# Differential heads: one fp32 product with the values in place of three on split operands

## The chip, the cores and the metric

The kernel runs on one core of a Trainium2 chip. The metric is the device time of one execution in microseconds. The core has a matrix engine (TensorE, PE in the profile; its weight loads have a row of their own, PEld), a vector engine (VectorE, DVE), a scalar engine (ScalarE, ACT), GpSimd (POOL) and a queue engine (SyncE, SP). Each works off its own list of instructions in order, and they wait for one another on semaphores.

## What is computed

A decoder block on x of 2048 x 1024 in fp32: RMSNorm, one input projection, two kinds of causal attention side by side, an output projection, and an MLP. There are 8 forgetting heads ("fox" below) of width 64 and 4 differential heads ("diff" below) with two score matrices each and values of width 128. The part that the change touches, from the reference:

```python
s = jnp.einsum('bqhnd,bkhnd->bhnqk', q_i, k).astype(jnp.float32) * scale
s = s + bias[None, :, None]
s = jnp.where(mask, s, -jnp.inf)
p = jax.nn.softmax(s, axis=-1)
a = p[:, :, 0] - lam * p[:, :, 1]
o = jnp.einsum('bhqk,bkhd->bqhd', a.astype(v.dtype), v)
o = rmsnorm(o, g_sub) * (1.0 - lam_init)
```

## The kernel before

There are four stages: the projection (to about 575 us of the profiled execution), the attention (to about 1376 us), the output projection and the MLP. fp32 products are made on TensorE from operands in the type fp32r: a number is split into a high part `hi`, which is the number copied into an fp32r tile, and a low part `lo`, the difference; the product is hi by hi, hi by lo and lo by hi, and each of the three is one matmul instruction.

The projection (`project`) makes a job for every 128 x 512 piece of its output. ScalarE copies the piece out of PSUM as `hi` (L534), VectorE subtracts to get `lo` (L598), and ScalarE's queue stores both. For the values there are 16 jobs of fox heads and 16 of diff heads; `vals` holds 256 columns for each row of a head, hi in the first 128 and lo in the other 128 for a diff head.

The attention (`attend`) goes through 8 units, fox and diff in turn: one unit is two fox heads or one diff head. A unit is cut into blocks of 512 queries (J = 0 to 3; a diff unit takes them in the order 1, 3, 2, 0), and a block needs keys up to its own end. For each block and each 128 queries the steps are

- score: TensorE, queries by keys into one of two PSUM buffers `at_ps_s` (L1462, the mask L1465, L1468);
- max: VectorE, the negated row maximum (L1361), and where a row has over 1024 keys the smaller of two (L1365) and on ScalarE a correction (L1293);
- exp: ScalarE, into `at_probs` (L1313); the score buffer is free after that;
- in diff blocks chain and mix: VectorE works out the factor of the second softmax (L1382 to L1390), and the second matrix is scaled and added to the first on VectorE (L1399, L1404), or on GpSimd (L1235 to L1251), or by ScalarE and GpSimd (L1320, L1322, L1222, L1226);
- turn: TensorE transposes 128 keys of up to 512 queries into one of the three PSUM buffers of the ring `at_ps_t`, in up to four matmuls of 128 columns (L1486);
- hi: ScalarE copies the turned tile into one of the four tiles `at_p_hi` (L1331);
- lo: VectorE subtracts, into `at_p_lo` (L1370); this also gives the ring's buffer back (semaphore `x_free`);
- pv: TensorE multiplies with the values into `at_ps_o`: two matmuls in a fox block (L1501, L1502), three in a diff block (L1504, L1505, L1506), all of up to 512 columns.

At the end of a diff block ScalarE squares the output (L1346), TensorE takes the mean with four matmuls of one column in fp32 (var, L1513), which take a place of the same ring, and VectorE (L1434, o_var) gives that place back. There are 480 turned tiles, 320 of fox blocks and 160 of diff blocks; the 160 are 112 of 512 queries and 16 each of 384, 256 and 128.

The order of all this is not written by hand. `attention_steps` hands each step to `Walk` with an engine, a holding time, a time to its result, an urgency and what it waits for; `Walk.order` lists them as the engines would come to them. A step's holding time is a number of us per column: 0.0009 for the pv of a fox block, 0.00135 for that of a diff block. The list is made once, when the program is built; on the chip each engine follows it in order.

## Time and profile before

| | |
|---|---|
| median of 3 runs | 2805.71 us (2801.96 to 2806.47) |
| the profiled execution | 2801.12 us |
| its span | 2799.4 us |
| granted TensorE clock, mean | 0.998 |
| TensorE busy over the span | 97% |
| VectorE busy over the span | 63% |
| ScalarE busy over the span | 48% |

The profile gives, for one execution, the busy time of each engine in each stretch, groups of equal instructions with their mean duration and the idle time before them with what ended it, and lists of waits. The duration of a matmul in it runs from its start to the arrival of its last result, so matmuls overlap in the records: what one costs the engine is the distance from its start to the start of the next.

### The profile page before, as it was taken

Reading aid. Unit: us, or ns where it says so; the run is one execution under the profiler, and the core shown is the slowest. Engines: PE = TensorE matmul, PEld = TensorE weight load, DVE = VectorE, ACT = ScalarE, POOL = GpSimd, SP = SyncE. Lnnn points to the kernel's source line nnn. Section 1 sums busy time; section 2 is a strip of 40 time slices with the busy share of each in tenths; the row PEclk is TensorE's granted clock in tenths of the full one; section 3 lists DMA queues with packets and bytes.
Section 4 is the critical chain, followed back from the end, with each engine's and each line's share of the span. In section 5 each row is a group of like instructions: output and inputs, shape, how many; then the busy total and the mean of one; then the engine's idle time right before and its main releaser. Section 6 shows DMA issues by size and latency. Waiting matters only on the chain.

```text
span 2799.4 us, 36795 instructions
## 1 busy us (share of the span) xinstructions
PE 2725.3 (97%) x13362; PEld 2253.3 (80%) x13362; DVE 1756.6 (63%) x2495; ACT 1344.5 (48%) x2413; POOL 629.6 (22%) x558
## 2 busy tenths in 40 slices
PE   8999999989999999999999999999999999999998
PEld 6888888878787787877788788888888888888887
DVE  6211111169889889899846778887777544435567
ACT  5121111168788788788523545464444433322233
POOL 5220021026746646556411100000000000000012
PEclk9999999999999999999999999999999999999999
DMA  5443343464434514414346755565345555546566
GB/s 190 131 153 101 104 136 113 144 148 98 105 83 97 128 52 118 123 41 120 106 128 217 260 204 199 186 237 201 134 149 196 180 186 209 185 159 224 203 219 240
DMA packets 287660, 434.49 MB, mean 155 GB/s; under 512 B 19648, under 2 KB 134592, under 8 KB 287488
## 3 DMA queue, kind: packets, MB, share of 16 engines
q1 hardware_dynamic: 241664, 368.41, 42.4%
q10 hardware_dynamic: 45056, 63.05, 6.2%
q8 instruction: 101, 1.65, 0.2%
q0 software_dynamic: 768, 0.79, 0.1%
q14 instruction: 71, 0.58, 0.1%
HBM read 280.27 MB, written 151.91 MB: 154 GB/s over the span
## 4 chain that ended last, share of the span: by engine, by line
PE 68%; DVE 5%; ACT 4%; issue 3%; POOL 0%; ACTq 0%; POOLq 0%; DVEq 0%
PE ml_ps L2845 7%; PE ml_ps L2843 7%; PE ml_ps L2844 7%; PE ml_ps L2813 7%; PE ml_ps L2815 7%; PE ml_ps L2816 7%; PE at_ps_t L1486 5%; PE at_ps_s L1462 4%; PE at_ps_s L1468 3%; PE mo_acc L1801 2%; PE mo_acc L1803 2%; PE mo_acc L1802 2%; PE at_ps_o L1501 2%; PE at_ps_o L1502 2%; ACT at_probs L1313 2%
## 5 line engine op out<-in xcount | busy, mean ns | idle before, releaser
L1361 DVE TENSOR_REDUCE at_nmax<-at_ps_s 128x1 f32<-128x1024 f32 (+7 forms) x384 | 346.6, 906 | 37.0 <-PE at_ps_s L1468 34.8
L2813 PE MATMUL ml_ps<-ml_h_hiM,ml_w_hi 128*128 128x512 f32 x896 | 349.1, 390 | 1.0 <-DVE ml_t L2635 0.9
L2816 PE MATMUL ml_ps<-ml_h_hiM,ml_w_lo 128*128 128x512 f32 x896 | 348.7, 389 | 0.0
L2815 PE MATMUL ml_ps<-ml_h_loM,ml_w_hi 128*128 128x512 f32 x896 | 348.7, 389 | 0.0
L2845 PE MATMUL ml_ps<-ml_b_hi,ml_a_lo 128*128 128x512 f32 x896 | 348.6, 389 | 0.0
L2844 PE MATMUL ml_ps<-ml_b_lo,ml_a_hi 128*128 128x512 f32 x896 | 348.6, 389 | 0.0
L2843 PE MATMUL ml_ps<-ml_b_hi,ml_a_hi 128*128 128x512 f32 x896 | 348.6, 389 | 0.0
L598 DVE SCALAR_TENSOR_TENSOR pj_out_sb<-pj_acc,pj_out_sb 128x512 fp32r<-128x512 f32 x96 | 66.4, 691 | 424.1 <-ACT pj_out_sb L534 424.1
L1370 DVE TENSOR_TENSOR at_p_lo<-at_ps_t,at_p_hi 128x512 fp32r<-128x512 f32 x480 | 280.0, 604 | 35.8 <-ACT at_p_hi L1331 32.7
L1331 ACT ACTIVATE at_p_hi<-at_ps_t 128x512 fp32r<-128x512 f32 x480 | 248.5, 533 | 87.6 <-PE at_ps_t L1486 48.0
L2490 POOL TENSOR_SCALAR ml_ss<-ml_ss 128x1 f32<-128x1 f32 x16 | 17.6, 1099 | 1183.7 <-ACT ml_junk L2583 1183.4
L1486 PE MATMUL at_ps_t<-at_ident_r,at_probs 128*128 128x128 f32 x1632 | 249.7, 275 | 14.9 <-DVE at_p_lo L1370 8.1
L534 ACT ACTIVATE pj_out_sb<-pj_acc 128x512 fp32r<-128x512 f32 x96 | 57.4, 598 | 422.8 <-PE pj_acc L705 268.8
L1313 ACT ACTIVATE at_probs<-at_ps_s,at_nmax 128x1024 f32<-128x1024 f32 (+7 forms) x256 | 237.4, 927 | 42.3 <-DVE at_nmax L1361 37.5
L1486 PEld LDWEIGHTS at_ps_t<-at_ident_r,at_probs 128*128 128x128 f32 x1632 | 193.8, 141 | 57.9 <-DVE at_p_lo L1370 16.0
L1462 PE MATMUL at_ps_s<-at_k,at_q 128*128 128x512 f32 (+3 forms) x640 | 211.5, 395 | 18.2 <-ACT at_probs L1313 14.4
L1215 POOL TENSOR_TENSOR at_probs<-at_probs,at_corr 128x1024 f32<-128x1024 f32 x96 | 181.9, 1894 | 152.8 <-ACT at_corr L1293 152.8
L2270 ACT ACTIVATE ml_b_hi<-ml_b_raw 128x1024 fp32r<-128x1024 f32 x56 | 59.4, 1061 | 307.2 <-issue 164.9
L1468 PE MATMUL at_ps_s<-at_k,at_q 128*128 128x512 f32 (+3 forms) x640 | 203.6, 383 | 0.0
L2813 PEld LDWEIGHTS ml_ps<-ml_h_hiM,ml_w_hi 128*128 128x128 f32 x896 | 168.2, 188 | 37.2 <-issue 1.7
L2125 ACT ACTIVATE ml_w_hi<-ml_w_sum 128x1024 fp32r<-128x1024 f32 x80 | 84.8, 1061 | 234.0 <-DVE ml_w_sum L2107 233.0
L2816 PEld LDWEIGHTS ml_ps<-ml_h_hiM,ml_w_lo 128*128 128x128 f32 x896 | 168.2, 188 | 35.0
(264 smaller groups left out, 5981.3 us busy)
## 6 DMA issues: line engine op xcount, KB each, us to landing
ml_a_raw<-ua SPq DMA_DIRECT2D x112, 512.0 KB, 3.9
qk<-pj_out_sb ACTq DMA_DIRECT2D x64, 512.0 KB, 2.8
ml_w_raw<-in_w_up_dram SPq DMA_DIRECT2D x64, 512.0 KB, 5.1
ua<-ml_t SPq DMA_DIRECT2D x128, 256.0 KB, 2.6
ml_b_raw<-in_w_down_dram SPq DMA_DIRECT2D x56, 512.0 KB, 4.9
at_q<-qk SPq DMA_DIRECT2D x96, 256.0 KB
at_k<-qk SPq DMA_DIRECT2D x96, 256.0 KB
ua<-ml_x SPq DMA_DIRECT2D x96, 256.0 KB, 2.6
```

The source lines that it names most:

```text
L1313: act.activation(out, ps_s[:, sc.g % 2, 0:sc.width], ACT.Exp, bias=bias, accum_out=rsum[:, par, sc.a, s, sc.part:sc.part + 1]).then_inc(ex ...
L1361: dve.tensor_reduce(nmax[:, par, sc.a, s, sc.part:sc.part + 1], ps_s[:, sc.g % 2, 0:sc.width], AX.X, ALU.max, negate=True).then_inc(maxed, 1)
L1370: dve.tensor_tensor(p_lo[:, t.n % PRING, t.off:512], ps_t[:, at % TRING, t.off:512], f32(p_hi[:, t.n % PRING, t.off:512]), ALU.subtract).t ...
L1462: pe.matmul(ps_s[:, sc.g % 2, at:at + width], q2[:, n, sc.s, q], k2[:, slot, sc.s, 0:width], start=True, stop=False)
L1468: last = pe.matmul(ps_s[:, sc.g % 2, at:at + width], q1[:, n, sc.s, q], k1[:, slot, sc.s, 0:width], start=False, stop=True)
L1486: last = pe.transpose(ps_t[:, at % TRING, a * P:(a + 1) * P], probs[:, key:key + P], ident)
L2813: pe.matmul(to, hi, h_hi[m][:, k, :], start=begins and k == 0, stop=False, skip_group_check=not begins)
L2815: pe.matmul(to, hi, h_lo[m][:, k, :], start=False, stop=False, skip_group_check=not begins)
L2816: last = pe.matmul(to, lo, h_hi[m][:, k, :], start=False, stop=k == 3, skip_group_check=not begins)
L2843: pe.matmul(to, hi, b_hi[b % 4][:, k, :], start=begin, stop=False)
L2844: pe.matmul(to, hi, b_lo[b % 4][:, k, :], start=False, stop=False)
L2845: last = pe.matmul(to, lo, b_hi[b % 4][:, k, :], start=False, stop=end)
```

## The change

In the diff blocks the turned probabilities are copied once, by ScalarE, in plain fp32 into a tile `p_whole`, which lies where `p_lo` lies. The step lo is left out there, so the ring's buffer is given back by ScalarE's copy (`hi_ready`). The product with the values is one matmul instruction in fp32 on the fp32 values instead of three in fp32r. The values of the diff heads are no longer split in the projection: VectorE copies a piece out of PSUM whole, ScalarE does nothing for it, and half as many bytes are stored and loaded. Fox blocks keep both parts. Two semaphores now tell of a free ring buffer, and the waits are counted apart (`hi_at`, `x_no`). In the planner the diff step lo is gone, and the holding time of the diff pv is 0.0018 us a column instead of 0.00135.

```diff
+def split(job):
+
+    return job.what == "qk" or (job.what == "val" and job.n == FOX)
...
+        with ExitStack() as shared:
+            r = Room(nc, shared, "atw")
+            r.sb("p_hi_place", [P, 4, 512])
+            self.p_whole = r.sb("p_whole", [P, 4, 512])
...
+                    used = 256 if job.n == FOX else P
+                    act.dma_start(vals[job.n, :, job.rb * P:(job.rb + 1) * P, 0:used].rearrange("i p c -> p i c"),
+                                  src.rearrange("p (i c) -> p i c", c=256)[:, :, 0:used]).then_inc(stored[job.out % OR], 16)
...
+                elif not split(job):
+                    dve.wait_ge(multiplied, m + 1)
+                    dve.wait_ge(stored[job.out % OR], 16 * (job.out // OR))
+                    dve.tensor_copy(f32(out_view(job, 0)), acc_view(job)).then_inc(evacuated, 1)
...
-            ring.append(("lo", t))
+            ready = ("lo", t) if fox else ("hi", t)
+            ring.append(ready)
...
-            walk.step("lo", t, "DVE", 0.07 + 0.00104 * width, at + RUSH["lo"], [("hi", t)], 0.15 + 0.00104 * width, line="ring")
-            cost = (0.0009 if fox else 0.00135) * width
+            if fox:
+                walk.step("lo", t, "DVE", 0.07 + 0.00104 * width, at + RUSH["lo"], [("hi", t)], 0.15 + 0.00104 * width,
+                          line="ring")
+            cost = (0.0009 if fox else 0.0018) * width
...
-                    act.activation(p_hi[:, t.n % PRING, t.off:512], ps_t[:, at % TRING, t.off:512], ACT.Copy)\
-                       .then_inc(hi_ready, 1)
...
+                    to = (p_whole if blocks[t.b].kind == DIFF else p_hi)[:, t.n % PRING, t.off:512]
+                    act.activation(to, ps_t[:, at % TRING, t.off:512], ACT.Copy).then_inc(hi_ready, 1)
...
+            def wait_free(at):
+                if at in hi_at:
+                    pe.wait_ge(hi_ready, hi_at[at])
+                else:
+                    pe.wait_ge(x_free, x_no[at])
...
-                        pe.matmul(out, v[:, 0:P], p_hi[:, ring, t.off:512], start=start, stop=False)
-                        pe.matmul(out, v[:, P:2 * P], p_hi[:, ring, t.off:512], start=False, stop=False)
-                        last = pe.matmul(out, v[:, 0:P], p_lo[:, ring, t.off:512], start=False, stop=t.end)
+                        last = pe.matmul(out, f32(v[:, 0:P]), p_whole[:, ring, t.off:512], start=start, stop=t.end)
```

The planner lists the steps of a diff unit in another order with this. On TensorE, in the second diff unit, from the mean of the first finished block (`at_mean`) on, before the change; `at_ps_s` are scores, `at_ps_t` turned tiles, `at_ps_o` the product with the values:

```order
L1486 MATMUL at_ps_t<-at_ident_r,at_probs 128x128 x12
L1513 MATMUL at_ps_t<-at_mean,at_o_sq 128x1 x4
L1462 MATMUL at_ps_s<-at_k,at_q 128x512 x2
L1468 MATMUL at_ps_s<-at_k,at_q 128x512 x2
L1486 MATMUL at_ps_t<-at_ident_r,at_probs 128x128 x4
L1462 MATMUL at_ps_s<-at_k,at_q 128x384
L1465 MATMUL at_ps_s<-at_mask_q,at_ident_r 128x128
L1468 MATMUL at_ps_s<-at_k,at_q 128x384
L1486 MATMUL at_ps_t<-at_ident_r,at_probs 128x128 x4
L1504 MATMUL at_ps_o<-at_p_hi,at_v_sb 128x512
L1505 MATMUL at_ps_o<-at_p_hi,at_v_sb 128x512
L1506 MATMUL at_ps_o<-at_p_lo,at_v_sb 128x512
```

The same place in the changed kernel:

```order
L1522 MATMUL at_ps_t<-at_ident_r,at_probs 128x128 x12
L1547 MATMUL at_ps_t<-at_mean,at_o_sq 128x1 x4
L1540 MATMUL at_ps_o<-atw_p_whole,at_v_sb 128x512
L1522 MATMUL at_ps_t<-at_ident_r,at_probs 128x128 x11
L1540 MATMUL at_ps_o<-atw_p_whole,at_v_sb 128x512
L1498 MATMUL at_ps_s<-at_k,at_q 128x512 x2
L1504 MATMUL at_ps_s<-at_k,at_q 128x512 x2
L1498 MATMUL at_ps_s<-at_k,at_q 128x384
L1501 MATMUL at_ps_s<-at_mask_q,at_ident_r 128x128
L1504 MATMUL at_ps_s<-at_k,at_q 128x384
```

One product and three more turned tiles now stand ahead of the two scores. On VectorE, at the same block's `at_var`, before and after the change:

```order
L1370 TENSOR_TENSOR at_p_lo<-at_ps_t,at_p_hi 128x512
L1361 TENSOR_REDUCE at_nmax<-at_ps_s 128x1
L1365 TENSOR_REDUCE at_top<-at_nmax 128x1
L1370 TENSOR_TENSOR at_p_lo<-at_ps_t,at_p_hi 128x512 x2
L1361 TENSOR_REDUCE at_nmax<-at_ps_s 128x1 x2
L1365 TENSOR_REDUCE at_top<-at_nmax 128x1
L1434 SCALAR_TENSOR_TENSOR at_var<-at_squares,at_ps_t 128x4
```

With the change, at that place:

```order
L1420 TENSOR_SCALAR at_factor<-at_factor,at_corr 128x1
L1393 TENSOR_REDUCE at_nmax<-at_ps_s 128x1 x2
L1397 TENSOR_REDUCE at_top<-at_nmax 128x1
L1464 SCALAR_TENSOR_TENSOR at_var<-at_squares,at_ps_t 128x4
```

The three subtractions are gone, and the maxima stand one behind the other.

## Rows read from the trace of the kernel before

**Rows 1.** Busy us by stretch; columns: stretch, its length, PE, PEld, DVE, ACT, POOL, PEclk, DMA

```profile
450.00:560.00 110.00, 110.00 (x487) 91.10 (x486) 13.83 (x20) 11.96 (x20) 8.37 (x3) 1.00 0.40 125
800.00:900.00 100.00, 96.29 (x573) 79.42 (x572) 92.98 (x156) 86.81 (x185) 57.50 (x43) 1.00 0.32 76
900.00:1000.00 100.00, 93.04 (x568) 77.58 (x568) 86.83 (x180) 77.21 (x181) 58.49 (x46) 1.00 0.47 118
```

**Rows 2.** The same view, short stretches of one diff unit's products with the values

```profile
904.00:912.00 8.00, 6.62 (x38) 5.29 (x38) 6.99 (x15) 7.70 (x16) 5.53 (x4) 1.00 0.22 66
912.00:920.00 8.00, 7.36 (x39) 5.70 (x38) 7.72 (x16) 7.01 (x16) 5.32 (x5) 1.00 0.54 143
926.00:932.00 6.00, 4.91 (x34) 4.29 (x33) 5.41 (x15) 4.71 (x10) 4.83 (x4) 1.00 0.00 0
...
944.00:950.00 6.00, 5.96 (x35) 4.82 (x34) 5.68 (x14) 4.99 (x14) 5.68 (x4) 1.00 0.34 85
950.00:956.00 6.00, 4.86 (x27) 3.74 (x26) 5.56 (x14) 2.58 (x8) 3.50 (x5) 1.00 1.04 230
...
968.00:974.00 6.00, 6.00 (x36) 5.01 (x35) 4.40 (x8) 4.32 (x14) 0.00 (x0) 1.00 1.02 244
```

**Rows 3.** Waits in 904:986; engine, line waited for: us in total, times, longest us

```profile
PE at_ps_s L1462 <- ACT at_probs L1313: 2.5, 5, 1.2
...
PE at_ps_t L1513 <- DVE at_p_lo L1370: 1.6, 2, 1.1
...
PE at_ps_t L1486 <- DVE at_probs L1404: 1.1, 1, 1.1
```

**Rows 4.** PE in order of time, four pieces; columns: start us, us, engine, line, operation

```profile
922.19 0.22 PE L1465 MATMUL at_ps_s<-at_mask_q,at_ident_r 128*128 128x128 f32 x1
922.25 0.45 PE L1468 MATMUL at_ps_s<-at_k,at_q 128*128 128x512 f32 x1
...
925.27 1.47 PE L1486 MATMUL at_ps_t<-at_ident_r,at_probs 128*128 128x128 f32 x12
...
935.80 0.40 PE L1504 MATMUL at_ps_o<-at_p_hi,at_v_sb 128*128 128x512 f32 x1
936.03 0.39 PE L1505 MATMUL at_ps_o<-at_p_hi,at_v_sb 128*128 128x512 f32 x1
936.26 0.40 PE L1506 MATMUL at_ps_o<-at_p_lo,at_v_sb 128*128 128x512 f32 x1
```

**Rows 5.** PE in order of time: one diff block's narrow products, and a mean

```profile
1372.96 0.34 PE L1504 MATMUL at_ps_o<-at_p_hi,at_v_sb 128*128 128x384 f32 x1
...
1373.50 0.28 PE L1504 MATMUL at_ps_o<-at_p_hi,at_v_sb 128*128 128x256 f32 x1
...
1373.86 0.22 PE L1504 MATMUL at_ps_o<-at_p_hi,at_v_sb 128*128 128x128 f32 x1
...
1374.14 0.62 PE L1530 MATMUL at_ps_t<-at_ident_r,at_row 128*128 128x128 f32 x4
1374.99 1.05 PE L1513 MATMUL at_ps_t<-at_mean,at_o_sq 128*128 128x1 f32 x8 [0.23 <-ACT at_o_sq L1346]
```

**Rows 6.** Groups of instructions in 560:1400; count, then busy us, mean ns, idle before

```profile
L1504 PE MATMUL at_ps_o<-at_p_hi,at_v_sb 128*128 128x512 f32 x112 | 49.5, 442 | 0.1
L1513 PE MATMUL at_ps_t<-at_mean,at_o_sq 128*128 128x1 f32 x128 | 16.0, 246 | 7.0 <-DVE at_p_lo L1370 6.3 <-ACT at_o_sq L1346 0.7
```

**Rows 7.** The page's costliest groups: the copies, the subtractions, the projection's evacuation

```profile
L598 DVE SCALAR_TENSOR_TENSOR pj_out_sb<-pj_acc,pj_out_sb 128x512 fp32r<-128x512 f32 x96 | 66.4, 691 | 424.1 <-ACT pj_out_sb L534 424.1
L1370 DVE TENSOR_TENSOR at_p_lo<-at_ps_t,at_p_hi 128x512 fp32r<-128x512 f32 x480 | 280.0, 604 | 35.8 <-ACT at_p_hi L1331 32.7
L1331 ACT ACTIVATE at_p_hi<-at_ps_t 128x512 fp32r<-128x512 f32 x480 | 248.5, 533 | 87.6 <-PE at_ps_t L1486 48.0
```

**Rows 8.** DMA issues: count, KB each, median us to landing

```profile
vals<-pj_out_sb ACTq DMA_DIRECT2D x32, 512.0 KB, 2.9
at_v_sb<-vals SPq DMA_DIRECT2D x32, 512.0 KB, 3.9
```

More of the change, by code:

```diff
@@ L221, in project @@
         splits_after[m].append(z)
-    hi_no = {m: sum(1 for job in jobs[:m + 1] if job.what in ("qk", "val")) for m in range(len(jobs))}
+    hi_no = {m: sum(1 for job in jobs[:m + 1] if split(job)) for m in range(len(jobs))}
     carry_job = next(m for m, job in enumerate(jobs) if job.what == "carry")
@@ L529, in _ @@
                 if job.out is not None:
-                    if job.what != "logit":
+                    if split(job):
                         act.wait_ge(multiplied, m + 1)
@@ L1048, in attend @@
             ring += 1
+    hi_no, hi_at, x_no, his, frees = {}, {}, {}, 0, 0
+    for (what, arg), at in ring_at.items():
+        if what == "turn":
+            his += 1
+            hi_no[arg.n] = his
+        if what == "turn" and blocks[arg.b].kind == DIFF:
+            hi_at[at] = his
+        else:
+            frees += 1
+            x_no[at] = frees
     last_turn = {t.b: t for t in turns}
@@ L1082, in attend @@
         k1, k2, q1, q2, p_hi, p_lo = keep.k1, keep.k2, keep.q1, keep.q2, keep.p_hi, keep.p_lo
+        p_whole = keep.p_whole
         k_loaded, q_loaded = keep.k_loaded, keep.q_loaded
@@ L1130, in attend @@
         last_turned = max(turns, key=lambda t: ring_at["turn", t])
+        last_copy = max(n for n, (what, arg) in enumerate(steps) if what in ("hi", "lo") and arg is last_turned)
         last_spread = max(pairs, key=lambda pair: ring_at["spread", pair[0].qb])[0].qb
@@ L1176, in sync @@
                         sp.wait_ge(p_used, max(t.n for t in turns if blocks[t.b].u == held and t.j // 4 == p) + 1)
[L1177 to L1178 removed]
+                    used = 256 if u % 2 == FOX else P
+                    sp.dma_start(f32(v_sb[:, k_slot(u, p), :, 0:used]),
+                                 vals[u % 2, u // 2, 512 * p:512 * p + 512, 0:used].rearrange("(t k) c -> k t c", k=P))\
                       .then_inc(v_loaded[k_slot(u, p)], 16)
@@ L1288, in scalar @@
             first_hi = next(arg for what, arg in steps if what == "hi")
-            for what, arg in steps:
+            for n, (what, arg) in enumerate(steps):
+                if n == last_copy + 1:
+                    then()
                 if what == "corr":
@@ L1330, in scalar @@
                         act.wait_ge(p_used, t.n - PRING + 1)
-                    act.activation(p_hi[:, t.n % PRING, t.off:512], ps_t[:, at % TRING, t.off:512], ACT.Copy)\
-                       .then_inc(hi_ready, 1)
-                    if t is last_turned:
-                        then()
+                    to = (p_whole if blocks[t.b].kind == DIFF else p_hi)[:, t.n % PRING, t.off:512]
+                    act.activation(to, ps_t[:, at % TRING, t.off:512], ACT.Copy).then_inc(hi_ready, 1)
                 elif what == "o_half":
@@ L1355, in link @@
                     dve.wait_ge(chained, links[0])
-            for what, arg in steps:
+            for n, (what, arg) in enumerate(steps):
+                if n == last_copy + 1:
+                    then()
                 if what == "max":
@@ L1368, in vector @@
                     t, at = arg, ring_at["turn", arg]
-                    dve.wait_ge(hi_ready, t.n + 1)
+                    dve.wait_ge(hi_ready, hi_no[t.n])
                     dve.tensor_tensor(p_lo[:, t.n % PRING, t.off:512], ps_t[:, at % TRING, t.off:512],
                                       f32(p_hi[:, t.n % PRING, t.off:512]), ALU.subtract).then_inc(x_free, 1)
-                    if t is last_turned:
-                        then()
                 elif what == "chain":
@@ L1531, in tensor @@
                     last.then_inc(x_ready, 1)
-        return Attention(sync, gpsimd, scalar, vector, tensor, len(scores), ring_at["turn", last_turned] + 1, ring, scored,
+        return Attention(sync, gpsimd, scalar, vector, tensor, len(scores), ring_at["turn", last_turned] + 1, frees, scored,
                          exped, x_ready, x_free, p_used, o_free)
```

21 lines of the change are left out of this document (9 added, 12 removed).

## The prediction

> **What bounds the kernel now.** I read the busy time by stretch first, since the change touches two places only: the evacuation of the diff values in the projection, and the diff units of the attention. In the projection the matrix engine is busy for all 110 us of a stretch in which VectorE is busy for 13.83 and ScalarE for 11.96 [rows 1]: there only TensorE's work counts, and the change leaves it as it is. The attention repeats every 200 us, one fox and one diff unit. Its fox half (800 to 900 us) has PE 96.29, DVE 92.98, ACT 86.81; its diff half (900 to 1000 us) 93.04, 86.83, 77.21 [rows 1]. So no engine has much room, and TensorE has least.
>
> Inside the diff half the reader is to see three kinds of stretches [rows 2]. From 904 to 920 us TensorE is idle by 2.0 of 16 us while ScalarE (7.70 of 8) and then VectorE (7.72 of 8) are full: the loop of score, max and exp sets the pace. From 926 to 932 and from 950 to 956 TensorE loses 1.1 us each. From 944 to 950 and from 968 to 974, and in all from 938 to 986 but for some 1.6 us, TensorE is full: there its own work is the time. The list of waits names what it waited for over 904 to 986 us: 2.5 us for ScalarE's exp, 1.6 us where a mean waits for the subtraction `p_lo`, 1.1 us for VectorE's mix, 5.2 us in all [rows 3]. That is a small store of idle time, and it is what the change can win on TensorE's side.
>
> **The price of the product before.** Three fp32r matmuls of 512 columns start at 935.80, 936.03 and 936.26 [rows 4]: 0.231 us apart, 0.693 us for the three. The narrow ones start 0.54 us apart for the three of 384 columns, 0.36 for 256 (1373.50 to 1373.86) and 0.28 for 128 (1373.86 to 1374.14) [rows 5]. A diff unit has 28 full turned tiles (a quarter of the 112 in [rows 6]) and 4 of each narrow width: 28 x 0.693 + 4 x (0.54 + 0.36 + 0.28) = 19.4 + 4.7 = 24.1 us.
>
> **The price of the product after.** No row has an fp32 matmul of this width, so it is bounded. First, how many pieces: the mean is the one fp32 product in the attention that is no transposition. The code issues 16 x 4 = 64 of them, and the trace has 128 [rows 6], eight for each group of four [rows 5]. So one fp32 matmul is two pairs of a weight load and a matmul, and three fp32r matmuls become two pieces. The question is what a piece of 512 columns takes.
>
> - The low end: a piece goes as fast as an fp32r matmul, 0.231 us. Two are 0.46 us and a unit is 16 us, 8 us less than now, 32 us over the four units.
> - The nearest row for an fp32 operand that moves: 128 columns of it in a transposition. Twelve of these take 1.47 us, of which the last record is 0.27: 1.20 / 11 = 0.109 us each [rows 4]. An fp32r matmul of 128 columns has its follower 0.06 us behind it (922.19 to 922.25) [rows 4]. At 0.109 us per 128 columns a piece of 512 is 0.436 and two are 0.872 us. Then a unit is 28 x 0.872 + 4 x (0.654 + 0.436 + 0.218) = 24.4 + 5.2 = 29.6 us: 5.5 us more than now, 22 us over four units.
> - The high end: each piece also waits for its own load, another 0.11 us, which is what a piece of one column takes in the mean ((1.05 - 0.25) / 7 = 0.114 [rows 5]). That is 1.09 us for a full tile, some 38.5 us a unit, 14.4 us more than now and 57 us over four.
>
> The transposition's 0.109 could be its weight load alone, since the one-column piece takes as long; that keeps the low end alive. I take 0.872: it is the row with the same type and the same kind of operand, and halving the pace on full fp32 fits a split in two pieces better than two full-precision operands at the price of two fp32r passes would. So TensorE gets **22 us** more work.
>
> The Trainium skill, in "FP8 and Floating Point Precision", section TensorE Precision Notes, says that true fp32 takes four passes through the array. At the spacing of the fp32r rows, four would be 0.924 us for a full tile, and my estimate by that page is 7.5 us a unit, 30 us over four; no run here shows it yet.
>
> **What of it lies on the path.** From 938 us on, where most of a unit's products with the values stand, TensorE is full, so a longer product moves all behind it. Ahead of that TensorE waits at times, but for other engines that are waited for after the product as well; the product is not what fills those waits. I count the 22 us whole and look for relief apart.
>
> **What goes.** VectorE loses 160 subtractions. The group of 480 is busy for 280.0 us [rows 7]; a third is 93 us, 23 us of the 87 that VectorE is busy in a diff half. By itself this is off TensorE's path; it counts through the waits. The mean's wait of 1.6 us a unit ends with `p_lo`, since the ring's place comes back with ScalarE's copy: I take all of it. The waits for the mix and for exp, 1.1 + 2.5 us, end partly on VectorE's backlog (it is busy for 5.68 of 6 us just before the wait for the mix [rows 2]) and partly on ScalarE and on the length of the chain. I take a quarter, 0.9 us. Together 2.5 us a unit, **10 us** over four. What is late next is TensorE itself. The bounds are 0 and 5.2 us a unit, 0 and 21 us.
>
> **What is nothing.** ScalarE's 160 copies stay, at 533 ns on average [rows 7]; they write plain fp32 with the same bytes. In the projection, 16 of ScalarE's copies and 16 of VectorE's 96 subtractions of 691 ns [rows 7] become 16 copies by VectorE of about the same length; cover is the full TensorE [rows 1], and with that gone each would cost no more than now. 16 stores and 16 loads of the 32 each [rows 8] shrink from 512 to 256 KB; no wait of TensorE in [rows 3] is for a load. `p_whole` lies over `p_lo`, but ScalarE waits for the product four tiles back already. The list puts a product and three more turned tiles ahead of two scores at the mean. Eleven transpositions and one product are 11 x 0.109 + 0.87 = 2.1 us by which that score comes later, which is exp's loop starved for VectorE and ScalarE once a unit; scores stand closer together later, so it can come back as waits of under 1 us. I leave it in the range.
>
> **Sum.** 22 - 10 = +12 us. On the profiled execution (2801.12 us, span 2799.4) that is 2813; on the median of the three runs, 4.6 us above it, **2817.7**.
>
> **Rivals.**
>
> 1. *VectorE was the brake* (ends faster or equal). With 23 of 87 us gone from VectorE, all 5.2 us of named waits fall, and also the short ones that a matmul record hides (a record of 0.40 us against a spacing of 0.23 covers 0.17 us; a dozen such places are 2 us a unit). Then 5.5 - 7.2 = -1.7 us a unit, 2799; with only the named waits gone, +1 us, 2807. For it: DVE 7.72 of 8 at 912 to 920 us. Against: TensorE is full for most of 938 to 986 us whatever VectorE does. It decides where relief is over 5.5 us a unit. I put it at 2796 to 2808.
> 2. *An fp32 piece is as fast as an fp32r one* (faster). -32 us on TensorE, of which, with VectorE and ScalarE next in line, I'd see most, and the relief is then partly the same time: 2765 to 2785. Against: the 0.109 row.
> 3. *The loads of fp32 weights are not hidden* (slower still). +57 - 12 = +45: 2840 to 2865. Against: loads hide behind every 512-column matmul now, and a piece of 0.436 us hides 0.11 more easily.
> 4. *The fp32 view is run as one fp32r pass or the waits stay as they were*, so that nothing of this shows. The code asks for fp32 on both operands, and the order shows one matmul for three. About 2806.
>
> **Chances.** Forecast case (2808 to 2836): 0.60, of which 0.08 below 2811.3. Rival 1: 0.22, half faster and half the same. Rival 2: 0.07. Rival 3: 0.08. Rival 4: 0.03. A measurement of this kernel can tell 0.2%, 5.6 us, from no change, so faster (below 2800.1) is 0.11 + 0.07 = 0.18, the same 0.08 + 0.11 + 0.03 = 0.22, slower 0.60. The range goes from 2798 (most of rival 1) to 2836, which is the product at 7.5 us more a unit with no relief; rivals 2 and 3 are left out.
>
> **What would show it.** Pieces of the fp32 product 0.43 to 0.46 us apart, 320 of them; the diff half of a period longer by about 3 us while VectorE's busy time in it falls by about 23; no wait of the mean for VectorE; fox halves and the projection as long as before. Pieces at 0.23 us would make the forecast wrong at its largest term, waits of TensorE for exp that nearly vanish would make it wrong at the second.

## The result, and the profile after

The changed kernel takes 2814.01 us, the median of six runs from 2813.11 to 2822.95; the kernel before, beside it on the same chip, 2805.85 us (six runs, 2801.87 to 2806.47). The ratio is 1.004 with a 95% interval of 1.0028 to 1.0053: slower by 8 to 15 us, and in the profiled executions all of it is in the attention. The profiled execution took 2813.96 us, span 2812.2, at a mean granted clock of 0.996; that of before took 2801.12 us at 0.998.

First the busy time by stretch, kernel after; the columns are those of [rows 1]:

```profile
450.00:560.00 110.00, 110.00 (x487) 91.13 (x486) 13.82 (x20) 3.59 (x6) 8.40 (x3) 1.00 0.35 97
800.00:900.00 100.00, 95.72 (x572) 78.81 (x570) 92.48 (x155) 86.60 (x185) 54.79 (x42) 1.00 0.32 74
900.00:1000.00 100.00, 95.14 (x517) 70.65 (x516) 64.03 (x137) 75.13 (x179) 58.83 (x45) 1.00 0.43 105
```

Beside [rows 1], the projection is what it was: the matrix engine full, 110.00 of 110 with 487 matmuls, while ScalarE has 6 instructions where it had 20. The fox half is within 0.6 us on every engine but GpSimd. In the diff half VectorE falls from 86.83 to 64.03 us, the 23 us of the removed subtractions, and TensorE rises from 93.04 to 95.14.

The new product, in PE's order of time and as groups (count, then busy us, mean ns, idle before), kernel after:

```profile
971.20 1.02 PE L1540 MATMUL at_ps_o<-atw_p_whole,at_v_sb 128*128 128x512 f32 x2
...
1355.58 2.79 PE L1540 MATMUL at_ps_o<-atw_p_whole,at_v_sb 128*128 128x512 f32 x6
```

```profile
L1540 PE MATMUL at_ps_o<-atw_p_whole,at_v_sb 128*128 128x512 f32 x224 | 111.6, 600 | 0.0
...
L1547 PE MATMUL at_ps_t<-at_mean,at_o_sq 128*128 128x1 f32 x128 | 16.7, 252 | 1.6 <-ACT at_o_sq L1376 1.2 <-ACT atw_p_whole L1364 0.5
```

Six pieces in a row take 2.79 us, of which the last record is some 0.60: 2.19 / 5 = 0.438 us apart. Two alone take 1.02, which leaves 0.42 to 0.43. The 112 full tiles are 224 pieces, and with 32 of each narrow width they are 320. The mean (L1547) no longer waits for VectorE; in [rows 6] that was 6.3 of its 7.0 us.

The waits of TensorE from 560 us to the end of the attention (columns as in [rows 3]), first before, then after:

```profile
PE at_ps_s L1462 <- ACT at_probs L1313: 14.4, 29, 1.2
...
PE at_ps_t L1513 <- DVE at_p_lo L1370: 6.3, 8, 1.1
...
PE at_ps_t L1486 <- DVE at_probs L1404: 4.5, 4, 1.1
```

```profile
PE at_ps_s L1498 <- ACT at_probs L1345: 17.5, 28, 1.8
...
PE at_ps_t L1522 <- DVE at_probs L1434: 1.3, 3, 0.4
PE at_ps_t L1547 <- ACT at_o_sq L1376: 1.2, 2, 0.7
PE at_ps_t L1547 <- ACT atw_p_whole L1364: 0.5, 2, 0.2
```

The mean's wait went (6.3 to 0.5 for ScalarE's copy), the mix's nearly (4.5 to 1.3), and the waits for exp did not fall: they rose from 14.4 to 17.5 us, the longest from 1.2 to 1.8. That longest one has something behind it. PE's order of time, and then the stretches around it, kernel after:

```profile
1358.11 0.50 PE L1498 MATMUL at_ps_s<-at_k,at_q 128*128 128x512 f32 x1
...
1361.35 0.44 PE L1498 MATMUL at_ps_s<-at_k,at_q 128*128 128x384 f32 x1 [1.83 <-ACT at_probs L1345]
...
1363.17 1.73 PE L1522 MATMUL at_ps_t<-at_ident_r,at_probs 128*128 128x128 f32 x9 [0.43 <-DVE at_probs L1434]
```

```profile
1356.00:1360.00 4.00, 3.52 (x12) 1.76 (x10) 2.37 (x9) 2.25 (x6) 2.93 (x3) 1.00 0.84 266
1360.00:1363.00 3.00, 1.39 (x6) 0.94 (x6) 3.00 (x5) 1.45 (x4) 0.09 (x1) 1.00 1.01 328
1363.00:1370.00 7.00, 6.83 (x29) 5.71 (x30) 2.32 (x9) 2.76 (x9) 5.12 (x5) 0.55 0.04 10
```

At each diff unit the list now puts four masked scores in a row. After the second TensorE waits 1.83 us for exp, since scores have no room until exp has read one; the same wait of 1.83 us stands at 756, 958 and 1160 us, one in each unit, where before none is over 1.2. In the 3 us from 1360 TensorE is busy for 1.39, and then the granted clock is 0.55 over 7 us, which is its lower level (1.2 GHz instead of 2.4) but for the ends: nine transpositions take 1.73 us there, against 1.47 for twelve in [rows 4]. The kernel after has three stretches of this kind that before has not, near 620, 757 and 1363 us, of 3.4, 3.4 and 6.8 us; one near 575 us they share. They come up again in the experiments.

The whole bill of TensorE, one long stretch of each kernel, from 560 us to the first product of the output projection (1375.90 before, 1389.82 after):

```profile
560.00:1375.90 815.90, 766.57 (x4571) 635.47 (x4571) 718.87 (x1330) 656.51 (x1461) 459.95 (x351) 1.00 0.40 100
```

```profile
560.00:1389.80 829.80, 787.62 (x4412) 617.40 (x4411) 635.15 (x1170) 654.97 (x1459) 459.62 (x351) 0.99 0.38 92
```

Busy time grew by 787.6 - 766.6 = 21.0 us, idle time fell from 49.3 to 42.2, by 7.1, and together the attention is 13.9 us longer; the rest of the program takes 1.1 us less (2812.2 - 1389.8 = 1422.4 against 2799.4 - 1375.9 = 1423.5). That has the form of the forecast's sum, 22 less 10, with 21 less 7. Two things make the likeness look better than it is. The profiled run of before was one of the quick ones: 2801.12 us where the median is 2805.85, so of 12.8 us between the profiles 8.2 are left between the medians. And busy time counts the half-speed stretches as work. Which step costs what can't be had from these two traces; it takes kernels with one step each.

### The profile page after: what moved, and what is told of

It is laid out like the page before. It is cut to its first block, busy times and chain, and to the rows that moved or that the text cites. A ratio compares the mean times of both kernels' runs of the same rounds, so it can differ in the third digit from the quotient of the medians.

```text
span 2812.2 us, 36299 instructions
## 1 busy us (share of the span) xinstructions
PE 2746.5 (98%) x13202; PEld 2235.0 (79%) x13202; DVE 1672.3 (59%) x2335; ACT 1334.7 (47%) x2397; POOL 628.8 (22%) x558
## 4 chain that ended last, share of the span: by engine, by line
PE 68%; DVE 6%; ACT 3%; issue 2%; POOL 0%; ACTq 0%; POOLq 0%; DVEq 0%
PE ml_ps L2878 7%; PE ml_ps L2879 7%; PE ml_ps L2877 7%; PE ml_ps L2847 7%; PE ml_ps L2849 7%; PE ml_ps L2850 7%; PE at_ps_t L1522 5%; PE at_ps_s L1504 3%; PE at_ps_s L1498 3%; PE at_ps_o L1540 3%; DVE at_nmax L1393 2%; PE mo_acc L1835 2%; PE mo_acc L1837 2%; PE mo_acc L1836 2%; PE at_ps_o L1537 2%
## 5 line engine op out<-in xcount | busy, mean ns | idle before, releaser
L612 DVE SCALAR_TENSOR_TENSOR pj_out_sb<-pj_acc,pj_out_sb 128x512 fp32r<-128x512 f32 x80 | 55.3, 691 | 348.1 <-ACT pj_out_sb L544 348.1
L1498 PE MATMUL at_ps_s<-at_k,at_q 128*128 128x512 f32 (+3 forms) x640 | 228.0, 421 | 19.7 <-ACT at_probs L1345 17.5
L544 ACT ACTIVATE pj_out_sb<-pj_acc 128x512 fp32r<-128x512 f32 x80 | 47.8, 598 | 345.5 <-PE pj_acc L719 268.9
L1504 PE MATMUL at_ps_s<-at_k,at_q 128*128 128x512 f32 (+3 forms) x640 | 205.0, 385 | 0.0
L1402 DVE TENSOR_TENSOR at_p_lo<-at_ps_t,at_p_hi 128x512 fp32r<-128x512 f32 (+1 forms) x320 | 185.7, 603 | 20.0 <-ACT at_p_hi L1364 17.6
L2877 PEld LDWEIGHTS ml_ps<-ml_b_hi,ml_a_hi 128*128 128x128 f32 x896 | 168.2, 188 | 35.0
L2878 PEld LDWEIGHTS ml_ps<-ml_b_lo,ml_a_hi 128*128 128x128 f32 x896 | 168.2, 188 | 34.9
```

What stands on the lines that cost most here:

```text
L1402: dve.tensor_tensor(p_lo[:, t.n % PRING, t.off:512], ps_t[:, at % TRING, t.off:512], f32(p_hi[:, t.n % PRING, t.off:512]), ALU.subtract).t ...
L1498: pe.matmul(ps_s[:, sc.g % 2, at:at + width], q2[:, n, sc.s, q], k2[:, slot, sc.s, 0:width], start=True, stop=False)
L1504: last = pe.matmul(ps_s[:, sc.g % 2, at:at + width], q1[:, n, sc.s, q], k1[:, slot, sc.s, 0:width], start=False, stop=True)
L2877: pe.matmul(to, hi, b_hi[b % 4][:, k, :], start=begin, stop=False)
L2878: pe.matmul(to, hi, b_lo[b % 4][:, k, :], start=False, stop=False)
```

## The experiments

Each was timed beside the kernel before on the same chip. All changes are given against that kernel's median of the same batch (2804.6 to 2805.85 us), as are the intervals of the ratio. There are four batches: the changed kernel's own; e1 to e4; e5 to e7; e8 to e10. Kernels of different batches are compared by their changes. "Stretch" is the time from 560 us to the first product of the output projection, with TensorE's busy and idle part, from the view shown last:

| kernel | product of diff tiles | subtraction | order of the work | median us | change us | ratio, 95% | stretch, busy + idle |
|---|---|---|---|---|---|---|---|
| before | three fp32r | yes | before's | 2805 | | | 815.9 = 766.6 + 49.3 |
| after | one fp32 | no | its own | 2814.01 | +8.2 | 1.0028 to 1.0053 | 829.8 = 787.6 + 42.2 |
| e1_old_order | one fp32 | no | before's | 2811.72 | +6.8 | 1.0015 to 1.0034 | 827.4 = 784.9 + 42.5 |
| e2_three_no_lo | three fp32r | no | before's | 2797.78 | -7.2 | 0.9967 to 0.9985 | 814.6 = 768.7 + 45.9 |
| e3_fp32_with_lo | one fp32 | yes | before's | 2818.95 | +14.0 | 1.0040 to 1.0067 | 833.4 = 786.6 + 46.8 |
| e4_cost168 | one fp32 | no | number 0.00168 | 2829.53 | +24.6 | 1.0075 to 1.0102 | 844.4 = 797.0 + 47.4 |
| e5_tuned_list | one fp32 | no | searched for it | 2801.39 | -3.6 | 0.9978 to 0.9996 | 814.7 = 780.0 + 34.7 |
| e6_one_pass | one fp32r | no | before's | 2792.99 | -12.0 | 0.9939 to 0.9970 | 808.7 = 732.1 + 76.6 |
| e7_three_in_e4_order | three fp32r | yes | e4's | 2851.77 | +46.7 | 1.0150 to 1.0178 | 866.6 = 792.5 + 74.1 |
| e8_three_in_e4_order_no_lo | three fp32r | no | e4's | 2811.17 | +6.6 | 1.0015 to 1.0033 | 827.2 = 776.9 + 50.3 |
| e9_three_tuned_no_lo | three fp32r | no | e5's | 2795.84 | -8.8 | 0.9957 to 0.9980 | 810.5 = 769.0 + 41.5 |
| e10_before_retuned | three fp32r | yes | searched for it | 2805.26 | +0.7 | 0.9992 to 1.0010 | 821.6 = 773.9 + 47.7 |

The question was first: are price, relief and order three separate terms, and of what size?

**The changed kernel in before's order (e1_old_order).** The list is made as before, with the subtractions of diff tiles in it, and these are then struck from it:

```diff
-            ready = ("lo", t) if fox else ("hi", t)
+            ready = ("lo", t)
...
-            if fox:
-                walk.step("lo", t, "DVE", ...)
-            cost = (0.0009 if fox else 0.0018) * width
+            walk.step("lo", t, "DVE", ...)
+            cost = (0.0009 if fox else 0.00135) * width
...
-    return walk.order()
+    return [(what, arg) for what, arg in walk.order() if what != "lo" or blocks[arg.b].kind == FOX]
```

> The changed kernel, with the steps listed in the order of the kernel before: the planner still counts the diff subtraction and 0.00135 us a column, and the subtraction is then taken out of the list. Theory A (the sum: price of the fp32 product +21 us by the spacing of 0.43 us that the changed kernel's trace shows, relief of VectorE -10, order nothing): as the changed kernel, +9 to +13 us on the kernel before. Theory B (the waits of TensorE for exp rose from 14.4 to 17.5 us because the new list puts more between the scores; relief by itself is larger): +3 to +7 us. Theory C (the new order is what makes use of the relief): +15 to +20 us.

Measured +6.8 us, in the range of Theory B and below that of A; the next run shows that B's reason, a larger relief, does not hold either. Product and dropped subtraction together cost this much with no step moved. The new order adds 2.3 us between the medians (2814.01 against 2811.72) or 1.4 between the changes; the intervals, +4 to +10 and +8 to +15, settle no more than that it is small. In the table TensorE's idle time is the same (42.5 and 42.2 us) and the busy time 2.7 us more, which two falls of the clock, at 757 and 1363 us, can explain; near 620 us e1 has one too.

**The relief alone (e2_three_no_lo).** Order as in e1; the values are split and loaded whole, ScalarE writes the fp32r part, VectorE's subtraction is gone, and the three matmuls all run on the fp32r part, so the low part of the probabilities is left out of the result:

```diff
-                        last = pe.matmul(out, f32(v[:, 0:P]), p_whole[:, ring, t.off:512], start=start, stop=t.end)
+                        pe.matmul(out, v[:, 0:P], p_hi[:, ring, t.off:512], start=start, stop=False)
+                        pe.matmul(out, v[:, P:2 * P], p_hi[:, ring, t.off:512], start=False, stop=False)
+                        last = pe.matmul(out, v[:, 0:P], p_hi[:, ring, t.off:512], start=False, stop=t.end)
```

> The relief alone. Order, projection and the three fp32r matmuls of the kernel before, but in diff blocks VectorE does no subtraction and the third matmul reads the high part again, so TensorE's work is the same and the low part of the probabilities is left out of the product. ScalarE's copy gives the ring's buffer back. Theory A: -10 us. Theory B: -13 to -18. Theory C (the relief is nothing without a new order): -4 to 0. If VectorE was the brake of the diff half: below -20.

Measured -7.2 us, between the ranges of A and C: the relief is smaller than the forecast's and is there without a new order. Its diff half, and its waits for exp:

```profile
900.00:1000.00 100.00, 94.05 (x579) 79.17 (x578) 67.25 (x141) 78.69 (x185) 59.54 (x48) 1.00 0.45 118
```

```profile
PE at_ps_s L1497 <- ACT at_probs L1344: 15.9, 33, 1.2
...
PE at_ps_t L1521 <- DVE at_probs L1433: 5.6, 4, 1.4
```

VectorE has 20 us less to do in a diff half, and the waits for exp and for the mix are 15.9 and 5.6 us where they were 14.4 and 4.5. What went is the mean's wait for VectorE. With the list otherwise the same, less work on VectorE does not shorten the other two.

**The price alone (e3_fp32_with_lo).** Order as before; the product is the fp32 one, VectorE still subtracts (into a place that nobody reads) and a turned tile's place still comes back with the subtraction:

```diff
-        if what == "turn" and blocks[arg.b].kind == DIFF:
-            hi_at[at] = his
-        else:
-            frees += 1
-            x_no[at] = frees
+        frees += 1
+        x_no[at] = frees
...
+                    diff = blocks[t.b].kind == DIFF
+                    to, copy = (p_hi, p_whole) if diff else (p_lo, p_hi)
+                    dve.tensor_tensor(to[:, t.n % PRING, t.off:512], ps_t[:, at % TRING, t.off:512],
+                                      f32(copy[:, t.n % PRING, t.off:512]), ALU.subtract).then_inc(x_free, 1)
```

> The price alone. Order of the kernel before, one fp32 matmul for the diff product, but VectorE still makes the subtraction (nobody reads it) and the ring's buffer and the product wait for it as before. All of the 21 us on the path: +19 to +23 us. If part of the longer product lies in time in which TensorE waited anyway: +10 to +16 us, and then the relief cannot be as large as -10 in the changed kernel.

Measured +14.0 us, in the range for a product that lies partly in time in which TensorE waited anyway. Its waits at the mean and for exp:

```profile
PE at_ps_s L1496 <- ACT at_probs L1341: 13.1, 24, 1.2
...
PE at_ps_t L1545 <- DVE at_p_hi L1400: 6.3, 8, 1.1
PE at_ps_t L1520 <- DVE at_probs L1432: 5.0, 4, 1.2
```

The mean's 6.3 us are back in full. And the terms add: -7.2 + 14.0 = +6.8, which is e1. So there are two separate terms in this order, a relief of 7.2 us and a price of 14.0.

Yet the pieces are 0.43 us apart, and by that the product alone has grown by 21 us. In the table busy time goes from 768.7 (e2) to 784.9 (e1), +16.2 us, and idle time from 45.9 to 42.5, -3.4; from before to e3 it is +20.0 and -2.5. Some 3 us of the price are thus gaps that the longer product fills, and the profiled run of e3 was at the clock 0.995 and that of before at 0.998. The remainder is not placed: an fp32r record of 0.40 us at a spacing of 0.23 can lie over a short gap, which busy time then doesn't show. That is argued, not shown.

**Taking TensorE's work away (e6_one_pass).** e2 with one fp32r matmul in place of three, so also the values' low part is left out. If TensorE's work is what the time goes by, this gains most of the 63 us that it removes (2 x 0.45 ns x 69632 columns).

```diff
-                        pe.matmul(out, v[:, 0:P], p_hi[:, ring, t.off:512], start=start, stop=False)
-                        pe.matmul(out, v[:, P:2 * P], p_hi[:, ring, t.off:512], start=False, stop=False)
-                        last = pe.matmul(out, v[:, 0:P], p_hi[:, ring, t.off:512], start=False, stop=t.end)
+                        last = pe.matmul(out, v[:, 0:P], p_hi[:, ring, t.off:512], start=start, stop=t.end)
```

> As the run with the relief alone, but the diff product is one fp32r matmul of the high parts (the products with both low parts are left out). TensorE loses 2 x 0.45 ns x 69632 columns = 63 us of work against that run. If TensorE's work is the path in the diff half as it was for the dearer product (14 us of 21 to 23 were seen): -38 to -42 us on that run, some -46 on the kernel before. If all of it is: -63, some -70. If VectorE, ScalarE and GpSimd take over as the bound once TensorE has room: -15 to -25, some -22 to -32 on the kernel before.

Measured -12.0 us, 4.8 below e2: smaller than any theory had. The diff half and the waits:

```profile
900.00:1000.00 100.00, 86.24 (x498) 70.10 (x498) 68.38 (x141) 78.56 (x186) 59.33 (x47) 0.95 0.48 120
```

```profile
PE at_ps_s L1497 <- ACT at_probs L1344: 38.5, 67, 1.2
PE at_ps_t L1521 <- DVE at_probs L1433: 9.9, 4, 2.5
```

Part of the time that TensorE no longer works it waits: 76.6 us idle in place of 45.9, and exp alone takes 38.5. But its busy time fell by only 36.6 us (768.7 to 732.1), not by 63: what is left of its work runs slower. In the diff units the granted clock is at its lower level for 44 us (10.2 us in each of the first three units, near 754, 952 and 1150 us, and twice 6.8 in the fourth), where e2 has no such stretch. The executions of e6 have mean clocks of 0.989 to 0.992, those of e2 0.996 to 0.998. By the 1.9 us for each 0.001 that is worked out below, an estimate puts 13 us on this, so that at e2's clock the removed 63 us would have brought some 18; no run shows the two apart.

So the diff half is held on two sides. Make the product longer and two thirds of it show (14 of 21 us); make it shorter by three times as much and one part in thirteen does as measured, or some three in ten by the estimate at an equal clock. In this order TensorE is the bound upward; downward the loop of score, max and exp is right behind it, and the waiting brings the clock down.

**The planner's number (e4_cost168).** The new order is made with 0.0018 us a column for the product; two pieces of 0.43 for 512 columns are 0.00168. That number alone is changed:

```diff
-            cost = (0.0009 if fox else 0.0018) * width
+            cost = (0.0009 if fox else 0.00168) * width
```

> The changed kernel with one number of the planner changed: 0.00168 us a column for the diff product, what its trace shows (0.861 us for 512), in place of 0.0018. The list differs in a dozen places of each diff unit. If the order matters little (A): within 2 us of the changed kernel. If the time hangs on how scores are spread (B): 3 us or more away from it, either way.

Measured +24.6 us: a number that is nearer the truth gives an order that is 16 us worse. Waits for exp, and the stretches around the longest of them, with columns as above:

```profile
PE at_ps_s L1498 <- ACT at_probs L1345: 24.6, 33, 1.9
```

```profile
1162.00:1166.00 4.00, 2.12 (x11) 1.19 (x10) 2.78 (x6) 2.23 (x6) 3.53 (x2) 1.00 0.42 112
1166.00:1179.00 13.00, 11.31 (x44) 9.62 (x43) 6.03 (x16) 5.78 (x17) 5.33 (x6) 0.50 0.70 153
```

```profile
1165.04 0.47 PE L1498 MATMUL at_ps_s<-at_k,at_q 128*128 128x512 f32 x1 [1.88 <-ACT at_probs L1345]
...
1168.29 0.69 PE L1498 MATMUL at_ps_s<-at_k,at_q 128*128 128x384 f32 x1 [1.69 <-ACT at_probs L1345]
```

It is the place of the kernel after at 1361 us, and here it has two such waits and not one: 1.9 us ahead of the four masked scores and 1.7 to 1.9 us between the second and the third, within 3.5 us, in three of the four diff units. Behind the pair shown the granted clock is 0.50 for 13 us. Waiting costs once by itself and, where the clock falls behind it, a second time.

**Is it the order or the fp32 product in it? (e7, e8)** First with before's own product, three fp32r matmuls on both parts, in e4's order. The subtractions, which that list lacks, were put right behind their copies:

```diff
-    return walk.order()
+    listed = []
+    for what, arg in walk.order():
+        listed.append((what, arg))
+        if what == "hi" and blocks[arg.b].kind == DIFF:
+            listed.append(("lo", arg))
+    return listed
```

> The kernel before (three fp32r matmuls, the subtraction by VectorE, values split), but with its steps in the order of the run with 0.00168 us a column, each diff subtraction right behind its copy. Theory D (the order with its runs of six scores without a turned tile makes TensorE wait, the granted clock falls there, and that is the 15 us by which that run is above the changed kernel's list and the 18 above the old one): +12 to +20 us on the kernel before, granted clock 0.993 or lower. Theory E (the fp32 pieces are what lowers the clock or does not stand such an order): 0 to +5 us, granted clock 0.995 or more as in the kernel before.

Measured +46.7 us, 22 above e4 and beyond what was expected. It doesn't answer the question: the place of the subtractions was mine and not the planner's, and in VectorE's list they stand ahead of maxima that exp waits for. Waits for exp:

```profile
PE at_ps_s L1502 <- ACT at_probs L1349: 33.8, 48, 1.9
```

So the same order once more without them, that is e2's product (the low part of the probabilities left out) and e4's number. The edit is the three matmuls of e2 and the 0.00168 of e4.

> The order of the run with 0.00168 us a column, but with three fp32r matmuls on the high part and no diff subtraction (as in the run with the relief alone, the low part of the probabilities is left out of the product). It is that run with another order, and the 0.00168 run with a cheaper product. Theory D (the order makes the waits and the fall of the clock, whatever the product): 15 to 20 us above the run with the relief alone, so +8 to +13 on the kernel before, granted clock 0.992 or lower. Theory E (the fp32 pieces lower the clock): within 5 us of the run with the relief alone, -7 to -2, granted clock 0.996 or more.

Measured +6.6 us at a clock of 0.992, between the two theories' times but with the clock of D. Against e2, which differs in the order alone, that is +13.8 us: the order is bad with either product. Against e4, which differs in the product alone, the price is 24.6 - 6.6 = 18.0 us. And e7 less e8, 40 us, is what the subtractions cost where I had put them.

**An order made for the product (e5_tuned_list).** If order is worth 15 us, a good one should be worth some too. I drew other urgencies for the planner and kept one whose list has few runs of scores without a turned tile between them (the runs that e4 shows), with 0.00168 for the product:

```diff
-RUSH = {"score": -1.113, "max": -0.06, "corr": 0.71, "exp": 0.362, "fix": 0.648, "chain": -1.388,
-        "mix": 0.875, "turn": 0.08, "hi": 0.131, "lo": -0.136, "pv": 0.259}
-SPREAD, LEAD, EARLY = 1.186, 0.433, 1.624
+RUSH = {"score": -1.112, "max": -0.224, "corr": 0.551, "exp": 0.300, "fix": 0.363, "chain": -3.527, "mix": 1.585, "turn": 0.102, "hi": 0.146, "lo": -0.453, "pv": 0.256}
+SPREAD, LEAD, EARLY = 1.188, 0.431, 1.604
...
-            cost = (0.0009 if fox else 0.0018) * width
+            cost = (0.0009 if fox else 0.00168) * width
```

> The changed kernel with other urgencies in the planner (the eleven numbers of RUSH, SPREAD, LEAD and EARLY, and 0.00168 us a column), chosen so that turned tiles and scores of a diff unit stand more evenly: one run of six scores without a turned tile instead of five. If the order costs as theory D has it: 5 to 10 us below the changed kernel and at or below the run with the old order (+1 to +6 us on the kernel before). If the old order was already as good as any: +6 to +8.

Measured 2801.39 us, -3.6 against before and some 12 against the changed kernel, better than either expectation; interval 0.9978 to 0.9996, which is 1 to 6 us below before. It computes what the reference asks for. About half of its lead on before is clock (see below); of that on the changed kernel 7.5 us are less idle time. Its diff half, and its waits:

```profile
900.00:1000.00 100.00, 96.33 (x528) 71.94 (x527) 67.50 (x140) 77.56 (x181) 59.14 (x47) 1.00 0.45 113
```

```profile
PE at_ps_s L1497 <- ACT at_probs L1344: 8.4, 16, 1.1
...
PE at_ps_t L1521 <- DVE at_probs L1433: 3.3, 4, 0.8
```

The waits for exp are half of what they were (8.4 against 17.5 us), none over 1.1 us, idle time is 34.7 us in place of 42.2, and the half-speed stretches are those near 575 and 619 us alone.

**Whose gain is it? (e9, e10)** e9 is e2's product in e5's order, e10 is the kernel before with urgencies looked for in the same manner:

```diff
-RUSH = {"score": -1.113, "max": -0.06, ...}
-SPREAD, LEAD, EARLY = 1.186, 0.433, 1.624
+RUSH = {"score": -1.0965, "max": -0.1119, "corr": 0.3643, "exp": 0.3575, "fix": -1.8603, "chain": -0.9596, "mix": 0.6270, "turn": 0.0971, "hi": 0.1270, "lo": -0.1696, "pv": 0.2761}
+SPREAD, LEAD, EARLY = 1.3158, 0.4721, 2.4035
```

> The tuned order with three fp32r matmuls on the high part and no diff subtraction. Against the tuned run it gives the price of the fp32 product in that order. If the price is a matter of TensorE's work alone, 14 us as between the runs in the old order: -17 to -19 us on the kernel before. If the tuned order hides more of it (waits of TensorE for exp are down to 8.4 us there from 15.0, so there is less to hide in): 16 to 21 us and -20 to -24. If this order suits only the longer product: -5 to -10.

> Control for the tuned run: the kernel before, nothing changed but the planner's urgencies, chosen in the same way for it. If the gain of the tuned run belongs to the fp32 product with one copy: within 2 us of the kernel before. If any kernel of this family gains 7 us or more from such a choice: -5 us or more, and the changed kernel would then not be the faster one at its best order.

e9 measured -8.8 us: with three short matmuls this order is 1.6 us better than the old one (e2, -7.2), within what can be told, and with the fp32 product it is 10.4 better (e5 against e1). The price of the product in this order is 8.8 - 3.6 = 5.2 us, loosely held, since the intervals of the two changes (-12 to -6 and -6 to -1 us) touch. It fits the expectation by which this order suits only the longer product. e10 measured +0.7: the same search brings the kernel before nothing, though the mean's wait for the subtraction is 2.0 us there and no longer 6.3. So the gain of e5 belongs to the changed kernel. One search each, judged by a rule on the list, doesn't show that before has no better order.

**The clock, from the repeated runs.** Each run has its own mean granted clock. The 20 runs of the kernel before in the batch of e1 to e4, by their clock (it is given to three digits):

| mean clock | time, us |
|---|---|
| 0.998 | 2800.8 to 2801.1 |
| 0.997 | 2801.8 to 2803.5 |
| 0.996 | 2804.8 to 2806.2 |
| 0.995 | 2805.8 to 2807.2 |

That is about 1.9 us for each 0.001 (a straight line through the 20), with nothing in the code changed. The kernel after gives 2813.1 to 2814.1 at 0.996, 2816.9 at 0.995 and 2822.95 at 0.993, and e4 2825.2 to 2832.6 at 0.991 to 0.989. Compared at 0.996 after and before differ by 8 us as the medians do. e4's median is 15.5 us above that of after; of these, (0.996 - 0.990) x 1.9 / 0.001 = 11 us are clock by this estimate, and the table has another 5.2 us of idle time.

The same estimate moves other differences. e5's mean clock is 0.9969 and that of before in its batch 0.9960, so some 1.7 of its 3.6 us are clock. The prices of the product come closer together: e5 and e9 have 0.9969 and 0.9954, which makes the 5.2 us some 8 at one clock, and e4 and e8 have 0.9902 and 0.9919, which makes the 18.0 some 15; e1 and e2 are both at 0.997, and their 14 stay. It is an estimate from one kernel's runs, and the clock is itself in part a result of the order.

Not every idle place brings the clock down. The three twins of the wait at 1361 us, kernel after, with the stretch ahead of each and behind:

```profile
955.00:958.00 3.00, 1.29 (x7) 0.84 (x6) 2.53 (x8) 1.48 (x6) 0.79 (x2) 1.00 1.00 229
958.00:965.00 7.00, 6.22 (x41) 5.08 (x42) 4.58 (x12) 4.03 (x13) 4.49 (x5) 1.00 1.03 215
1157.00:1160.00 3.00, 1.17 (x6) 0.77 (x6) 2.89 (x9) 1.49 (x4) 0.41 (x2) 1.00 0.94 228
1160.00:1167.00 7.00, 6.35 (x43) 4.88 (x42) 4.21 (x12) 4.03 (x14) 4.88 (x5) 1.00 1.00 207
753.00:756.00 3.00, 1.18 (x7) 0.73 (x5) 2.64 (x8) 1.49 (x5) 0.68 (x2) 1.00 0.95 218
756.00:760.00 4.00, 3.99 (x18) 3.67 (x18) 3.05 (x7) 1.60 (x4) 1.69 (x2) 0.57 1.07 229
```

TensorE is busy for 1.2 to 1.3 of 3 us ahead of all of them; behind 958 and 1160 the clock stays at 1.00, behind 756 it is 0.57. Nor does it take a wait of 1.8 us. The first mean of the second diff unit waits 1.1 us for the subtraction in the kernel before and in e3 alike, and only in e3 the clock falls behind it. Before, then e3:

```profile
926.00:930.00 4.00, 2.91 (x22) 2.46 (x21) 3.44 (x11) 3.32 (x8) 2.83 (x2) 1.00 0.00 0
930.00:937.00 7.00, 6.87 (x40) 5.59 (x38) 6.12 (x15) 5.17 (x13) 6.50 (x5) 1.00 0.00 0
```

```profile
930.00:934.00 4.00, 2.92 (x25) 2.65 (x24) 3.86 (x11) 3.21 (x8) 2.46 (x3) 1.00 0.02 6
934.00:938.00 4.00, 4.00 (x17) 3.24 (x16) 3.05 (x6) 1.93 (x5) 4.00 (x3) 0.59 0.00 0
```

The longest falls shown so far stand behind two waits close together (13.7 us in e4) and behind a wait of 2.5 us for the mix (10.2 in e6), but what decides between two like places is open. If it can go either way from run to run, that would explain the spread of clocks in the table; no trace here shows one kernel twice.

## Why the prediction was right, point by point

The forecast was 2817.7 us, slower, within 2798 to 2836. It is 2814.01: the direction holds, and of +12 us on before's median there were +8.2. The terms, though, were both too large, and a third had been left out.

- **The pieces.** Right. Two pieces for each fp32 matmul, 320 in all, 0.43 us apart, 0.86 us for a full tile where 0.872 was taken from the transpositions. With the measured spacing a unit is 28 x 0.86 + 4 x (0.64 + 0.43 + 0.22) = 29.2 us, 5.1 more than before, 21 over four. The Trainium skill, in "FP8 and Floating Point Precision", section TensorE Precision Notes, counts four passes; two pieces of 0.43 us are four of 0.215, which fits beside the 0.231 of one fp32r matmul, though the trace shows only the two pieces and not the passes. My estimate from that page had used the fp32r rows' spacing of 0.231 and came to 30 us, 9 too many. The low end (0.23 a piece) and the high end (0.55) are both out.
- **What of it lies on the path.** The step that was mis-sized: "I count the 22 us whole", since "the product is not what fills those waits". TensorE does 21 us more work, but in the old order only 14.0 us of it show (e3, and e1 against e2, by two ways), 18 in e4's order and 5 in e5's (some 15 and 8 at one clock, by the estimate above). The product does fill some of the waits, and how much depends on the list: TensorE's idle time falls by 3.4 us in the old order (e2 to e1) and by 6.8 in e5's (e9 to e5). I had read "TensorE is full from 938 to 986" as a bound on both sides; e3 and e6 show that a fuller TensorE costs two thirds and that an emptier one brings little, since it then waits for exp and its clock falls.
- **What goes.** Mechanism right, size a little off: 10 forecast, 7.2 measured. The mean's wait goes in full, 6.3 to 0.5 us, as counted. The quarter of the waits for mix and exp does not: with the subtraction gone and nothing else (e2) they are 15.9 and 5.6 us, as long as before. VectorE's backlog was not what they ended on. "Waits for exp that nearly vanish" did not come.
- **The order.** Left in the range as "waits of under 1 us". It was the term that could have overturned the result: between the four orders tried for the same changed kernel lie 2801.4 and 2829.5 us, 28 us, more than either term of the sum. For the order as it was built it is small (e1 against after), so the sum held; this was not known when it was written. That scores standing closer together would come back as waits was right; place and size were not. At the place named, the first mean of a unit, TensorE does not wait at all (in the second diff unit not once from 929 to 957 us). The wait stands some 28 us later, between masked scores ahead of the unit's next mean, and it is 1.8 us, in one unit with 6.8 us at half clock behind it and in one with 3.4.
- **The granted clock.** Not priced at all. It took part of the 4.6 us between before's profiled run and its median, and the three new falls in after.
- **What was counted at nothing.** Right: in the projection 110.00 us of 110 as before, ScalarE's copies as long (598 ns for 512 columns), 16 copies by VectorE of 691 ns under a full TensorE, and the halved loads and stores in no wait. The page's group and the DMA issues of after, beside [rows 7] and [rows 8]:

```profile
L609 DVE COPY pj_out_sb<-pj_acc 128x512 f32<-128x512 f32 x16 | 11.1, 691 | 75.3 <-PE pj_acc L727 75.3
```

```profile
at_v_sb<-vals SPq DMA_DIRECT2D x16, 512.0 KB, 4.1
```

- **The rivals.** Rival 1, VectorE as the brake with -12 to -5 us for the whole, falls: 23 us off a diff half brought 7.2 us in four, and the one wait that went is the mean's for a subtraction. But its result, 2801 us, is what e5 reaches by the order. Rivals 2 and 3 fall with the spacing, rival 4 with the 320 pieces.

Both terms were too large, and they have opposite signs: 22 - 10 = 12 against 14.0 - 7.2 = 6.8, and 1 to 2 us of order on top. That the sum came out within 4 us is partly luck of this kind.

## What to carry to other kernels

Where two engines each are nearly full, price an edit in both directions: a stretch in which TensorE is 93% busy charged 14 us for 21 of added work and paid back 5 for 63 removed (some 18 by an estimate at an equal clock). When an instruction's length changes by a fifth in a list that a planner makes, try more than one list for it and look for runs of one kind of work that fill the buffers: the best and the worst order of the changed kernel lie 28 us apart, and the edit itself costs 7. And compare medians at one granted clock, since a profiled run can sit 4 us below it for nothing in the code.

## What the runs showed of the hardware

- An fp32 matmul of 128 x 128 by 512 columns is two records 0.43 us apart, 0.86 us in all, against 0.23 for an fp32r one, and it scales with the columns (0.22 us for the two of 128).
- Behind some waits of 1.1 to 2.5 us (e3, e6, e4, the kernel after) the granted clock fell to its lower level for 3.4 to 13.7 us; behind others of the same length it did not (958 and 1160 us of the kernel after). Nine transpositions took 1.73 us there, against 1.47 us for twelve. A mean clock lower by 0.001 goes with 1.9 us of this kernel.
- With 63 us of matmuls removed (e6) the clock fell in every diff unit, for 6.8 to 10.2 us at a time (0.95 over 900 to 1000 us, against 1.00 in e2), which gave back part of the gain, 13 us by an estimate.
